# Attention and tail of a three-layer kernel: ScalarE takes part of the normalising, a compressed branch in fewer VectorE operations, split tiles moved, the last down tile in quarters

## The chip, the cores and the metric

The program runs on one core of one Trainium2 chip. The metric is the device time of one execution in microseconds; the figure is the median of several runs. The core has a matrix engine (PE, TensorE), VectorE (DVE), ScalarE (ACT), GpSimd (POOL) and SyncE (SP), which only issues transfers here. Each engine runs its own list of instructions in order and waits on semaphores.

## The reference

A block of two layers (attention mixer, gated feed-forward) is followed by a third layer of another kind; 256 tokens, 1024 features, everything in float32.

```python
def hybrid_mixer(h, w_in, ...):
    ... = jnp.split(h @ w_in, IN_OFFSETS, axis=-1)
    o_a = nsa_mixer(...)      # compressed + selected + window attention, 5 heads
    o_b = dsa_mixer(...)      # 5 heads over the 64 keys that an indexer chose
    o_c = dilated_mixer(...)  # 6 heads
    return jnp.concatenate([o_a, o_b, o_c], axis=-1)
# in nsa_mixer
    hid = jax.nn.gelu(jnp.einsum('cbnf,cfh->cbnh', raw, cmp_w1))
    kv_cmp = jnp.einsum('cbnh,chd->cbnd', hid, cmp_w2)
    p_c, _ = masked_softmax(s_c, mask_c)
    o_cmp = jnp.einsum('bhtn,bnd->bthd', p_c, v_cmp)
    gs = jax.nn.sigmoid(g)
    return gs[..., 0:1] * o_cmp + gs[..., 1:2] * o_slc + gs[..., 2:3] * o_win
# the third layer ends with
    m = jnp.einsum('btf,fd->btd', jnp.square(jax.nn.relu(u @ w_up)), w_down)
    h = h + rms_norm(m, norm_mlp_post)
```

## The kernel before

**Weights.** 170 tiles of up to 128 x 2048 float32 are streamed by SP into four buffers `raw`. Each is split for PE: ScalarE copies it to `whi` (L1174, the high part, 1.9 us), and VectorE (L1599) or GpSimd (L2422, eight pieces of 256 columns) subtracts to get `wlo`. Three split tiles are held. `ahead(tile)` splits the tile two places further on in the stream, so a line such as `ahead(l, "in", 3, 1)` in ScalarE's program means the split of the first tile of the output projection. `on_pool` says which low parts GpSimd makes; in the attention these are the last input tiles and all four output tiles. SP loads into a buffer when both parts of the tile four places earlier are made. A product of float32 accuracy is three products: high x high, high x low, low x high; twelve of them (2.8 us) make half a tile for 128 tokens (`tokens_half`, L540 to L543).

**Attention of a layer** (PE's list in `attention`, with the same-named lists of ScalarE and VectorE). Work is cut in ten pairs of jobs; a job is a group of heads over 128 queries, job 2p + i being half i of pair p. Pairs 0 to 3 are the first mixer (`NS`, a selected and a window segment for each head), 4 to 6 the second (`DS`), 7 to 9 the third (`DI`). For pair p:

- `scores(p)` on PE: a bf16 product lays down the mask (L804), products of 64 rows add the scores (L810), in bank 0 for even and bank 1 for odd jobs. It waits until the exponentials of the job before have been read from the bank.
- `highest(p)` on VectorE (L1982): the negated maxima.
- `weights(p)` on ScalarE (L1322, L1318): exponentials out of the bank to SBUF (tiles `E` and `XN`), with their sums `den`.
- `divided(p)` on VectorE: reciprocal (L1994), product with the gate for `NS` (L1999), then one scaling for each segment (L2004).
- `turned(p)`: PE transposes the weights (L822) into banks 2 and 3; ScalarE (L1334) or VectorE (L2042) copies them out.
- `values(p)` on PE (L854).

Between these stand halves of input tiles (`part`), the transposition of queries and keys (`transposed`: PE L678, out by ScalarE L1217 or VectorE L1695; pairs 9 and 11 use bank 2, pairs 10 and 12 bank 3), the last value columns (`last_values`, 24 products of 256 columns, L900 to L902, and `last_values_turned`, L908), and the output projection (`out_half`), which needs the mixed values as high part (ScalarE, L1346) and low part (VectorE, `mixed`, L2033). The jobs' order on each engine is written out by hand in the source.

**Beside it** VectorE finds the chosen keys of the second mixer: `selection(t, a, b)` is b - a rounds of eight maxima (L1723) and their replacement (L1725); `select` must be over before `scores(4)`. The compressed branch is `gelu_in` (L1817 to L1823), a tanh on ScalarE (L1351), `gelu` (L1827 to L1832), `compressed` (L1839, L1840), the scores on PE (L880), `compressed_scores` (L1845 to L1853), an exponential (L1356) and `compressed_softmax` (L1858 to L1867). Its result is one more addend of `values`.

**The end.** The third layer's 16 down tiles accumulate in banks 4 to 7, one for each half of tokens t and half of columns n. For the last tile `down` runs t = 0 wholly, then t = 1, with both n in turn. ScalarE squares each bank with a sum (`post_square`, L1399), VectorE multiplies by a gain (L2050), sums (L2396), GpSimd takes the power -1/2 (L2431), VectorE adds to the stream (L2058), and SP stores. Layers 0 and 1 end with `down_quarter`, which finishes one bank at a time.

## Time and profile before

| | |
|---|---|
| median of 3 runs | 1069.06 us (1068.77 to 1070.2) |
| the profiled execution | 1067.52 us |
| its span, first to last instruction | 1066.2 us |
| granted TensorE clock over the span | 0.994 of full speed |
| PE busy | 1043.7 us, 98% of the span |
| VectorE, ScalarE, GpSimd busy | 779.5, 539.4, 242.3 us |
| attention of layer 0, of layer 1 | about 54 to 141 us, 376 to 464 us |

Profile rows give a start from the beginning of the span. Matmuls are pipelined, so that rows of PE overlap, and the time between two starts says more than a row's length. A bracket is the engine's idle time before the row, and what ended it.

### The profile page before, as it was taken

The page shows a single profiled execution, that of the slowest core. Times are in us where ns is not written, and L with a number is a line of the kernel's source. Part 1 is how long each engine was busy: PE and PEld are TensorE (multiplying, and loading weights), DVE is VectorE, ACT ScalarE, POOL GpSimd, SP SyncE. Part 2 cuts the span into 40 slices and gives each one's busy share as a digit, 9 for nine tenths or more (in the row PEclk, how much of TensorE's full clock was granted, in tenths as well). Part 3 has the DMA queues.
Part 4 walks back from the last instruction along what each step waited for, and adds up shares of the span by engine and source line. Part 5 has one row for each costly group of instructions (what it writes and reads, how often), then busy time and mean ns, then how long its engine had stood idle before and what let it go on. Part 6 is the DMA issues. An engine that isn't in the chain of part 4 may idle for free.

```text
span 1066.2 us, 14818 instructions
## 1 busy us (share of the span) xinstructions
PE 1043.7 (98%) x5722; PEld 863.9 (81%) x5722; DVE 779.5 (73%) x1256; ACT 539.4 (51%) x797; POOL 242.3 (23%) x335
## 2 busy tenths in 40 slices
PE   8999999999999999899999999999999999999997
PEld 6777788888888867688888888998788878888886
DVE  6987568788778887658877778988754558666665
ACT  5445565555555455556555546655434445434332
POOL 1262610000000271620000003128957630000000
PEclk9989999999999999999999999999999999999999
DMA  9351345645554351355655554443444555555531
GB/s 362 124 188 60 119 157 166 230 147 209 197 177 159 138 207 41 115 173 192 203 192 197 174 182 158 159 159 124 152 158 175 199 199 186 192 198 195 171 145 39
DMA packets 26709, 179.15 MB, mean 168 GB/s; under 512 B 2960, under 2 KB 2960, under 8 KB 6160
## 3 DMA queue, kind: packets, MB, share of 16 engines
q1 hardware_dynamic: 26640, 178.22, 47.4%
q8 instruction: 45, 0.74, 0.3%
q14 instruction: 24, 0.20, 0.1%
HBM read 177.16 MB, written 1.05 MB: 167 GB/s over the span
## 4 chain that ended last, share of the span: by engine, by line
PE 90%; DVE 7%; ACT 2%; issue 1%; DMA 1%; SPq 0%; DVEq 0%; ACTq 0%
PE pb L602 18%; PE pb L603 9%; PE pb L540 8%; PE pb L541 8%; PE pb L543 7%; PE pb L628 6%; PE pb L630 6%; PE pb L629 6%; PE pb L607 3%; PE pb L854 2%; PE pb L565 1%; PE pb L566 1%; PE pb L567 1%; PE pb L606 1%; PE pb L822 1%; PE pb L810 1%
## 5 line engine op out<-in xcount | busy, mean ns | idle before, releaser
L1599 DVE TENSOR_TENSOR wlo<-raw,whi 128x2048 fp32r<-128x2048 f32 x124 | 283.7, 2290 | 113.2 <-ACT whi L1174 113.1
L1174 ACT ACTIVATE whi<-raw 128x2048 fp32r<-128x2048 f32 (+1 forms) x165 | 305.0, 1853 | 70.8 <-PE pb L543 36.9
L602 PE MATMUL pb<-hb,whi 128*128 128x512 f32 x840 | 302.0, 399 | 0.9 <-DVE hb L1621 0.9
L2422 POOL TENSOR_TENSOR wlo<-raw,whi 128x256 fp32r<-128x256 f32 x284 | 215.4, 794 | 331.1 <-ACT whi L1174 331.0
L603 PE MATMUL pb<-hb,wlo 128*128 128x256 f32 x840 | 235.9, 281 | 0.0
L602 PEld LDWEIGHTS pb<-hb,whi 128*128 128x128 f32 x840 | 158.2, 188 | 35.1 <-issue 1.1
L603 PEld LDWEIGHTS pb<-hb,wlo 128*128 128x128 f32 x840 | 159.2, 190 | 5.1
L540 PE MATMUL pb<-whi,hb 128*128 128x512 f32 x384 | 156.4, 407 | 6.0 <-DVE hb L2033 1.6
L541 PE MATMUL pb<-wlo,hb 128*128 128x512 f32 x384 | 151.3, 394 | 0.0
L543 PE MATMUL pb<-whi,hb 128*128 128x512 f32 x364 | 143.5, 394 | 0.0
L628 PE MATMUL pb<-whi,gh 128*128 128x512 f32 x288 | 114.1, 396 | 0.0
L630 PE MATMUL pb<-whi,gl 128*128 128x512 f32 x288 | 114.0, 396 | 0.0
L629 PE MATMUL pb<-wlo,gh 128*128 128x512 f32 x288 | 114.0, 396 | 0.0
L2431 POOL TENSOR_TENSOR sm<-sm 128x1 f32<-128x1 f32 x12 | 8.5, 721 | 429.0 <-DVE sm L1607 243.6
L540 PEld LDWEIGHTS pb<-whi,hb 128*128 128x128 f32 x384 | 73.1, 190 | 28.4 <-issue 13.6
L541 PEld LDWEIGHTS pb<-wlo,hb 128*128 128x128 f32 x384 | 73.2, 191 | 14.1
L543 PEld LDWEIGHTS pb<-whi,hb 128*128 128x128 f32 x364 | 69.2, 190 | 15.0
L630 PEld LDWEIGHTS pb<-whi,gl 128*128 128x128 f32 x288 | 54.2, 188 | 13.0
L629 PEld LDWEIGHTS pb<-wlo,gh 128*128 128x128 f32 x288 | 54.2, 188 | 13.0
L628 PEld LDWEIGHTS pb<-whi,gh 128*128 128x128 f32 x288 | 54.2, 188 | 11.7 <-issue 0.3
L1305 ACT ACTIVATE gh<-th 128x512 fp32r<-128x512 f32 x22 | 13.9, 632 | 76.3 <-DVE th L1958 76.3
L607 PE MATMUL pb<-hb,whi 128*128 128x512 f32 x120 | 47.5, 396 | 0.0
(367 smaller groups left out, 1472.0 us busy)
## 6 DMA issues: line engine op xcount, KB each, us to landing
raw<-wst SPq DMA_DIRECT2D x160, 1024.0 KB, 4.8
raw<-wst SPq DMA_DIRECT2D x8, 512.0 KB, 3.5
gb<-gains SPq DMA_DIRECT2D x3, 512.0 KB, 5.8
X<-x SPq DMA_DIRECT2D x4, 256.0 KB, 6.8
out<-X SPq DMA_DIRECT2D x4, 256.0 KB, 2.0
PQ<-prm SPq DMA_DIRECT2D x1, 909.0 KB, 4.5
prmt<-prm SPq DMA_DIRECT2D x1, 547.0 KB, 5.8
raw<-wst SPq DMA_DIRECT2D x2, 256.0 KB, 6.9
```

Of the source, the lines that this page charges most:

```text
L540: e.matmul(o, high[:, s], wh[:, k, :], start=first and k == 0, stop=False)
L541: mm = e.matmul(o, high[:, s], wl[:, k, :], start=False, stop=False)
L543: mm = e.matmul(o, low[:, s], wh[:, k, :], start=False, stop=last and k == 3)
L602: e.matmul(both, wh[:, k, s], hb2[:, k, :, :].rearrange("p i q -> p (i q)"), start=k == 0, stop=False)
L603: e.matmul(high, wl[:, k, s], hh[:, k, :], start=False, stop=False)
L607: mm = e.matmul(both, wh[:, 7, s], hb2[:, 7, :, :].rearrange("p i q -> p (i q)"), start=False, stop=True)
L628: e.matmul(o, ah, wh[:, k, c], start=j == 0 and k == 0, stop=False)
L629: e.matmul(o, ah, wl[:, k, c], start=False, stop=False)
L630: mm = e.matmul(o, al, wh[:, k, c], start=False, stop=last and k == 1)
L1174: e.activation(whi[:, split_slot(m), 0:w], raw[:, m % RAW, 0:w], ACT.Copy).then_inc(*hi(m))
L1599: e.tensor_tensor(wlo[:, split_slot(m), 0:w], raw[:, m % RAW, 0:w], whi[:, split_slot(m), 0:w].bitcast(F32), ALU.subtract).then_inc(*lo_v(m))
L2422: g = e.tensor_tensor(wlo[:, split_slot(m), s], raw[:, m % RAW, s], whi[:, split_slot(m), s].bitcast(F32), ALU.subtract)
```

## The change

- `divided`: for the first mixer VectorE multiplies the sum by (1 + exp(-g)) and takes one reciprocal. Then for `NS` jobs 1, 2, 3, 5 and 7 (`norm_done`) ScalarE does the scalings, in a `divided(p)` of its own in its list; VectorE goes on with jobs 0, 4 and 6 and all others.
- Compressed branch: gelu's input in two fused operations that read the bank, clamp and subtraction in one (the sign is turned, the exponential has scale -1), clamp and gate in one. The gates' reciprocal (L1781) is gone.
- VectorE's rounds of selection stand at other places among these.
- In ScalarE's list the splits behind `ahead(l, "in", 3, 1)` and `ahead(l, "in", 5, 0)` stand later, and pair 5's exponentials stand around `turned(4)`, job 10's before, job 11's behind it.
- PE does `last_values` before `values(5)` and no longer behind `turned(6)`.
- The last down tile of the third layer runs through `down_quarter`, in the order (0,0), (0,1), (1,0), (1,1); the squares wait for their own quarter.

```diff
@@ -434,6 +434,11 @@
+        def norm_done(j):
...
+            return normed_a if jobs[j][0] == NS and (j % 2 or len(jobs[j][2]) == 1 and jobs[j][1] == 0) else normed
...
         def segments(j):
@@ -632,17 +638,19 @@
-                m = tile_at[l, "down", 10, 0]
+                j = LAST_DOWN[l]
+                m = tile_at[l, "down", j, 0]
                 wh, wl = (w.rearrange("p (k c) -> p k c", k=2) for w in parts(m))
...
                 for k in range(2):
-                    e.matmul(o, gh[:, 0, k, s], wh[:, k, c], start=False, stop=False)
-                    e.matmul(o, gh[:, 0, k, s], wl[:, k, c], start=False, stop=False)
-                    mm = e.matmul(o, gl[:, 0, k, s], wh[:, k, c], start=False, stop=k == 1)
+                    e.matmul(o, gh[:, j % 2, k, s], wh[:, k, c], start=False, stop=False)
+                    e.matmul(o, gh[:, j % 2, k, s], wl[:, k, c], start=False, stop=False)
+                    mm = e.matmul(o, gl[:, j % 2, k, s], wh[:, k, c], start=False, stop=k == 1)
                 mm.then_inc(*(used(m) if t and n else half_used(m, t, n)))
-                free[DOWNB[t, n]] = x_new[("down", l), t, n]
+                if l < 2:
+                    free[DOWNB[t, n]] = x_new[("down", l), t, n]
@@ -816,7 +824,7 @@
-                        q.wait_ge(*normed[l, j])
+                        q.wait_ge(*norm_done(j)[l, j])
@@ -952,10 +960,10 @@
                 scores(7)
+                last_values()
                 values(5)
...
                 free[4], free[5] = mix_hl[l, 0], mix_hl[l, 1]
-                last_values()
                 scores(8)
@@ -1153,7 +1161,9 @@
                         down(tile_at[2, "down", j - 1, 0], j - 1, False)
-                down(tile_at[2, "down", 15, 0], 15, True)
+                for t in range(2):
+                    for n in range(2):
+                        down_quarter(2, t, n)
@@ -1306,8 +1316,8 @@
             def attention(l, transposed, project):
-                def weights(p):
-                    for j in halves_of(p):
+                def weights(p, i=None):
+                    for j in halves_of(p) if i is None else halves_of(p)[i:i + 1]:
                         k, t, hs = jobs[j]
@@ -1323,6 +1333,17 @@
+                def divided(p):
+                    for j in halves_of(p):
+                        if norm_done(j) is normed:
+                            continue
+                        n = 128 * (jobs[j][1] + 1)
+                        q.wait_ge(*divisor[l, j])
+                        for i, s in enumerate(columns(j)):
+                            o = weights_at(j)[:, i * n:i * n + n]
+                            a = e.activation(o, o, ACT.Copy, scale=co[:, s:s + 1])
+                        a.then_inc(*normed_a(l, j))
...
                 def turned(p):
@@ -1351,31 +1372,35 @@
                 ahead(l, "in", 2, 1)
+                divided(0)
                 weights(1)
-                q.wait_ge(*cmp_v[l, "less max"])
-                e.activation(ce, ce, ACT.Exp).then_inc(*act(l, "ce"))
+                q.wait_ge(*cmp_v[l, "below max"])
+                e.activation(ce, ce, ACT.Exp, scale=-1.0).then_inc(*act(l, "ce"))
+                divided(1)
                 project(2, 0, 6)
...
                 ahead(l, "in", 3, 0)
+                divided(2)
                 q.wait_ge(*mm_ce[l])
...
                 transposed(9)
+                divided(3)
                 turned(2)
...
                 project(3, 1, 7)
-                ahead(l, "in", 3, 1)
-                weights(5)
+                weights(5, 0)
                 turned(4)
+                weights(5, 1)
                 transposed(11)
                 weights(6)
+                ahead(l, "in", 3, 1)
                 turned(5)
-                ahead(l, "in", 5, 0)
                 weights(7)
@@ -1383,6 +1408,7 @@
                 turned(6)
+                ahead(l, "in", 5, 0)
                 weights(8)
@@ -1578,7 +1604,7 @@
                     for c in range(2):
-                        post_square("post2", t, c, lambda t, n: (used if t else half_used)[tile_at[2, "down", 15, 0]])
+                        post_square("post2", t, c, lambda t, n: last_down(2, t, n))
@@ -1776,9 +1802,7 @@
                 q.wait_ge(*gate_exp[l])
-                e.tensor_scalar(gs, gs, 1.0, None, ALU.add).then_inc(*dve())
-                q.wait_ge(*q.prev)
-                e.reciprocal(gs, gs).then_inc(*dve(l, "gates"))
+                e.tensor_scalar(gs, gs, 1.0, None, ALU.add).then_inc(*dve(l, "gates"))
                 e.memset(E[:, 0:2, 0:272], 0.0).then_inc(*dve(l, "E zero"))
@@ -1813,17 +1837,17 @@
                 def gelu_in():
+                    hp = PB[4][:, 256:288]
                     q.wait_ge(*mm_kv[l, "hidden"])
-                    e.tensor_copy(hx, PB[4][:, 256:288]).then_inc(*cmp_v(l, "hx"))
+                    e.tensor_copy(hx, hp).then_inc(*cmp_v(l, "hx"))
                     q.wait_ge(*q.prev)
-                    e.tensor_tensor(h2, hx, hx, ALU.mult).then_inc(*dve())
+                    e.scalar_tensor_tensor(h2, hp, 0.044715, hx, ALU.mult, ALU.mult).then_inc(*dve())
                     q.wait_ge(*q.prev)
-                    e.tensor_scalar(h2, h2, 0.044715, 1.0, ALU.mult, ALU.add).then_inc(*dve())
-                    q.wait_ge(*q.prev)
-                    e.tensor_tensor(h2, h2, hx, ALU.mult).then_inc(*cmp_v(l, "gelu in"))
+                    e.scalar_tensor_tensor(h2, h2, 1.0, hp, ALU.add, ALU.mult).then_inc(*cmp_v(l, "gelu in"))
...
                     q.wait_ge(*tanh_h[l])
+                    q.wait_ge(*cmp_v[l, "hx"])
                     e.scalar_tensor_tensor(h3, h3, 1.0, hx, ALU.add, ALU.mult).then_inc(*dve())
@@ -1848,41 +1872,38 @@
                     q.wait_ge(*q.prev)
-                    e.tensor_scalar(cm, cm, -1e29, None, ALU.max).then_inc(*dve())
-                    q.wait_ge(*q.prev)
-                    e.tensor_tensor(cev, cev, cmv.unsqueeze(3).broadcast_to([128, 2, 5, 16]),
-                                    ALU.subtract).then_inc(*cmp_v(l, "less max"))
+                    e.scalar_tensor_tensor(cev, cmv.unsqueeze(3).broadcast_to([128, 2, 5, 16]), -1e29, cev, ALU.max,
+                                           ALU.subtract).then_inc(*cmp_v(l, "below max"))
...
                     q.wait_ge(*q.prev)
-                    e.tensor_scalar(cd, cd, 1e-30, None, ALU.max).then_inc(*dve())
+                    q.wait_ge(*dve[l, "gates"])
+                    e.scalar_tensor_tensor(cdv, cdv, 1e-30, g0[:, :, :, 0], ALU.max, ALU.mult).then_inc(*dve())
                     q.wait_ge(*q.prev)
...
                     q.wait_ge(*q.prev)
-                    q.wait_ge(*dve[l, "gates"])
-                    e.tensor_tensor(cdv, cdv, g0[:, :, :, 0], ALU.mult).then_inc(*dve())
-                    q.wait_ge(*q.prev)
                     e.tensor_tensor(cev, cev, cdv.unsqueeze(3).broadcast_to([128, 2, 5, 16]),
...
                 gelu_in()
+                selection(1, 2, 3)
                 highest(0)
                 gelu()
-                selection(1, 2, 3)
+                selection(1, 3, 4)
                 compressed()
                 divided(0)
-                selection(1, 3, 4)
                 highest(1)
                 compressed_scores()
+                divided(1)
                 selection(1, 4, 6)
-                divided(1)
                 compressed_softmax()
                 highest(2)
-                selection(1, 6, 8)
+                selection(1, 6, 7)
                 divided(2)
+                selection(1, 7, 8)
                 highest(3)
@@ -1989,15 +2010,19 @@
                             at_ = at_[0:1]
-                        cv_ = co[:, at_[0]:at_[-1] + 1]
+                        cv_, dv_ = co[:, at_[0]:at_[-1] + 1], den[:, at_[0]:at_[-1] + 1]
                         q.wait_ge(*exped[l, j])
-                        e.reciprocal(cv_, den[:, at_[0]:at_[-1] + 1]).then_inc(*dve())
+                        if k == NS:
+                            q.wait_ge(*dve[l, "gates"])
+                            e.tensor_tensor(cv_.rearrange("p (h b) -> p h b", b=2), dv_.rearrange("p (h b) -> p h b", b=2),
+                                            g0[:, t, hs[0]:hs[-1] + 1:2, 1:3], ALU.mult).then_inc(*dve())
+                            q.wait_ge(*q.prev)
+                            e.reciprocal(cv_, cv_).then_inc(*divisor(l, j))
+                            if norm_done(j) is normed_a:
+                                continue
+                        else:
+                            e.reciprocal(cv_, dv_).then_inc(*dve())
                         q.wait_ge(*q.prev)
-                        if k == NS:
-                            cw_ = cv_.rearrange("p (h b) -> p h b", b=2)
-                            q.wait_ge(*dve[l, "gates"])
-                            e.tensor_tensor(cw_, cw_, g0[:, t, hs[0]:hs[-1] + 1:2, 1:3], ALU.mult).then_inc(*dve())
-                            q.wait_ge(*q.prev)
                         w = 3 * n if k == DI else n
@@ -2386,10 +2411,8 @@
                 ahead(2, "down", 15, 0)
-                post_gain("post2", 0, 0, 48)
                 for t in range(2):
-                    if t:
-                        post_gain("post2", 1, 0, 48)
+                    post_gain("post2", t, 0, 48)
                     q.wait_ge(*squares["post2", t, 1])
...
                     zz = norm_of["post2"]
```

**ScalarE, the first two pairs of the attention, and what follows them.** L1322 (L1332 now) are exponentials, L1174 (L1184) a split, L1351 (L1372) the tanh, L1356 (L1378) the compressed exponential, L1209 (L1219) an eviction of a projection, L1344 the scaling. Before:

```order
L1322 ACTIVATE E,sm<-pb,sm 128x128 x8
L1174 ACTIVATE whi<-raw 128x2048
L1322 ACTIVATE E,sm<-pb,sm 128x128 x2
L1322 ACTIVATE E,sm<-pb,sm 128x256 x2
L1356 ACTIVATE sm<-sm 128x160
L1209 ACTIVATE PQ<-pb,sm 128x512 x2
```

With the change:

```order
L1332 ACTIVATE E,sm<-pb,sm 128x128 x8
L1184 ACTIVATE whi<-raw 128x2048
L1344 ACTIVATE E<-E,sm 128x128 x4
L1332 ACTIVATE E,sm<-pb,sm 128x128 x2
L1332 ACTIVATE E,sm<-pb,sm 128x256 x2
L1378 ACTIVATE sm<-sm 128x160
L1344 ACTIVATE E<-E,sm 128x128 x2
L1344 ACTIVATE E<-E,sm 128x256 x2
L1219 ACTIVATE PQ<-pb,sm 128x512 x2
```

Four scalings stand in front of the second pair's exponentials, four more in front of the two evictions.

**ScalarE, pairs 5 to 7.** L1334 (L1355) copies turned weights, L1217 (L1227) transposed queries and keys, L1382 (L1407) the last values, L1346 (L1367) makes the mixed values' high part. Before:

```order
L1174 ACTIVATE whi<-raw 128x2048
L1322 ACTIVATE XN,sm<-pb,sm 128x128 x5
L1334 ACTIVATE PT<-pb 128x512
L1217 ACTIVATE PQ<-pb 128x256 x2
L1322 ACTIVATE E,sm<-pb,sm 128x256
L1334 ACTIVATE XN<-pb 128x256
L1174 ACTIVATE whi<-raw 128x2048
L1322 ACTIVATE E,sm<-pb,sm 128x256 x4
L1382 ACTIVATE rl<-pb 64x256
L1346 ACTIVATE hb<-pb 128x2x256 x2
```

With the change:

```order
L1332 ACTIVATE XN,sm<-pb,sm 128x128 x2
L1355 ACTIVATE PT<-pb 128x512
L1332 ACTIVATE XN,sm<-pb,sm 128x128 x3
L1227 ACTIVATE PQ<-pb 128x256 x2
L1332 ACTIVATE E,sm<-pb,sm 128x256
L1184 ACTIVATE whi<-raw 128x2048
L1355 ACTIVATE XN<-pb 128x256
L1332 ACTIVATE E,sm<-pb,sm 128x256 x4
L1407 ACTIVATE rl<-pb 64x256
L1367 ACTIVATE hb<-pb 128x2x256 x2
L1355 ACTIVATE PT<-pb 128x256
L1184 ACTIVATE whi<-raw 128x2048
```

The first split moved from ahead of the five exponentials to behind the one of pair 6; they are two and three now, with the copy between; the second split went from pair 6 to behind the mixed values.

**PE, from pair 7's scores to the first output products.** Each engine row of L900 to L902 stands for one product of the last value columns; the rest of the 24 are alike. Before:

```order
L804 MATMUL pb<-mskt 128x512 x2
L810 MATMUL pb<-PQ 128x256 x4
L854 MATMUL pb<-XN,PQ 64x128 x5
L822 MATMUL pb<-prmt,E 128x128 x2
L900 MATMUL pb<-hb,whi 64x256
L901 MATMUL pb<-hb,whi 64x256
```

With the change:

```order
L812 MATMUL pb<-mskt 128x512 x2
L818 MATMUL pb<-PQ 128x256 x4
L908 MATMUL pb<-hb,whi 64x256
L909 MATMUL pb<-hb,whi 64x256
L910 MATMUL pb<-hb,wlo 64x256
```

The value products of pair 5 (L854) and the first turning of pair 6 (L822) stood ahead of the last value columns and now stand behind them.

## Rows read from the trace of the kernel before

**Rows 1.** The page's part 1: busy us, share, instructions of an engine.
```profile
PE 1043.7 (98%) x5722; PEld 863.9 (81%) x5722; DVE 779.5 (73%) x1256; ACT 539.4 (51%) x797; POOL 242.3 (23%) x335
```

**Rows 2.** Waits of PE by line and releaser: us in total, times, longest.
```profile
PE pb L804 <- ACT E L1322: 2.4, 4, 0.9
PE pb L822 <- DVE PQ L1695: 1.9, 2, 1.0
PE pb L540 <- DVE hb L2033: 1.6, 2, 0.8
...
PE pb L678 <- ACT PT L1334: 1.4, 2, 0.7
...
PE pb L804 <- ACT XN L1322: 1.0, 2, 0.5
```

**Rows 3.** Stretches of one us, PE alone: stretch, PE busy, granted clock, DMA share, GB/s.
```profile
66.00:67.00 1.00, 1.00 (x4) 0.92 0.95 393
73.00:74.00 1.00, 1.00 (x4) 0.66 0.97 123
391.00:392.00 1.00, 1.00 (x5) 0.56 0.00 0
394.00:395.00 1.00, 1.00 (x5) 0.74 0.00 0
```

**Rows 4.** Timeline of PE, attention of layer 1: start us, us, operation, idle before.
```profile
387.94 0.39 PE L804 MATMUL pb<-mskt 128*128 128x512 bf16 x1 [0.93 <-ACT E L1322]
...
427.79 1.06 PE L678 MATMUL pb<-prmt,PQ 128*128 128x128 f32 x8 [0.71 <-ACT PT L1334]
...
432.06 0.61 PE L804 MATMUL pb<-mskt 128*128 128x512 bf16 x2 [0.32 <-ACT E L1322]
...
438.33 0.28 PE L908 MATMUL pb<-prmt,rl 64*128 64x64 f32 x2
...
439.40 0.47 PE L540 MATMUL pb<-whi,hb 128*128 128x512 f32 x1 [0.79 <-DVE hb L2033]
```

**Rows 5.** Timeline of DVE in the same attention, same columns.
```profile
382.22 0.75 DVE L1819 TENSOR_TENSOR sm<-sm 128x32 f32<-128x32 f32 x1
...
383.69 0.67 DVE L1823 TENSOR_TENSOR sm<-sm 128x32 f32<-128x32 f32 x1
...
385.47 0.27 DVE L1827 SCALAR_TENSOR_TENSOR sm<-sm 128x32 f32<-128x32 f32 x1
...
386.17 0.43 DVE L1723 MAX8 sm<-sc 128x8 f32<-128x256 f32 x1
...
386.71 0.41 DVE L1725 MATCH_REPLACE8 sc<-sm,sc 128x256 f32<-128x256 f32 x1
...
388.20 0.87 DVE L2004 TENSOR_SCALAR E<-E,sm 128x128 f32<-128x128 f32 x4
...
389.40 1.85 DVE L2004 TENSOR_SCALAR E<-E,sm 128x128 f32<-128x128 f32 x4
...
428.47 1.93 DVE L2004 TENSOR_SCALAR XN<-XN,sm 128x128 f32<-128x128 f32 x3
```

**Rows 6.** Timeline of ACT in the same attention.
```profile
384.99 0.37 ACT L1322 ACTIVATE E<-pb,sm 128x128 f32<-128x128 f32 x1 [0.37 <-DVE sm L1982]
...
387.74 1.95 ACT L1174 ACTIVATE whi<-raw 128x2048 fp32r<-128x2048 f32 x1
...
392.60 0.37 ACT L1322 ACTIVATE E<-pb,sm 128x128 f32<-128x128 f32 x1 [2.92 <-DVE sm L1982]
...
427.04 0.61 ACT L1334 ACTIVATE PT<-pb 128x512 f32<-128x512 f32 x1
```

**Rows 7.** Timeline of POOL in the same attention.
```profile
426.17 5.52 POOL L2422 TENSOR_TENSOR wlo<-raw,whi 128x256 fp32r<-128x256 f32 x8
```

**Rows 8.** Timeline of ACT at the end of the program.
```profile
1060.40 0.60 ACT L1399 ACTIVATE E<-pb 128x512 f32<-128x512 f32 x1 [1.53 <-PE pb L630]
```

11 lines of the change are left out of this document (6 added, 5 removed).

## The prediction

> **What bounds the kernel now.** I read the page's busy shares first, then who waited for whom on PE, then the granted clock in stretches of one microsecond, then the timelines of the engines in the attention of the second layer. PE is busy for 1043.7 of 1066.2 us [rows 1], so only three things are to be had: its idle time, the time at half clock, and what follows its last product. The change touches no product's size.
>
> Idle time of PE that the change can reach stands in [rows 2]: 2.4 us for the exponentials in E before score products, 1.9 for the copy of a transposed key pair (L1695), 1.6 for the low half of the mixed values (L2033), 1.4 for a weight copy (L1334), 1.0 for exponentials in XN. The first four occur in both layers and at the same places; the last is layer 1 alone. That is 8.3 us in all.
>
> The clock: it is 0.92 in the slice from 66 us and 0.66 in the one from 73 [rows 3], and 0.50 between. Two levels, 2.4 and 1.2 GHz, give the ends: from 66.84 to 73.68, so 6.8 us at half speed in layer 0, which cost 3.4. In layer 1 (0.56 and 0.74) it is 391.1 to 394.5, 3.4 us, cost 1.7. Together 5.1 us. Ahead of both falls PE had waited 0.81 and 0.93 us at the second score job, and did narrow products.
>
> **The change part by part.** All sums are against the profiled execution, 1067.5 us. That one is 1.5 us under the median of the runs shown, 1069.1; the two differ by about what one more fall of the clock costs.
>
> *The gelu's input, and the round of selection ahead of it.* VectorE now has three operations of 32 columns behind the copy, from 382.22 to 384.27 [rows 5]: 2.05 us at 0.64 to 0.75 each, while GpSimd splits a tile. A fused operation of the same width took 0.27 at 385.47 (L1827). After the change there are two fused ones that read PSUM: 0.6 us with gaps. The bounds are 0.27 and 0.75 each, so 0.6 to 1.6; I take 0.6, since the row of the same operation is nearest. One round of selection (L1723 and L1725, 386.17 to the end of the row at 386.71 and a short gap) costs 0.96 and now stands ahead of the maxima. They begin at 383.8 and not 384.27. The eight exponentials, 384.99 to 387.74 [rows 6], then end 0.5 earlier, and the second score job waits 0.3 to 0.45 and not 0.81 and 0.93 [rows 4]. **Gain 0.5 a layer, 1.0.** With the fused operations at 0.75 it is a loss of 0.5 a layer.
>
> *VectorE gives up five of its scaling jobs to ScalarE.* These are jobs 1, 2, 3, 5 and 7, and with them goes row 389.40, 1.85 us for four 128x128 scalings; the same four took 0.87 at 388.20 [rows 5]. Between the two GpSimd began a split. After the change VectorE reaches the maxima of the third pair of jobs some 3.5 us sooner: 1.85 of job 1, about 2 of jobs 2 and 3, less what stays. It only matters where PE waited for it. In layer 1 that is the 1.0 us for exponentials in XN [rows 2]; in layer 0 PE was late itself, at half clock. **Gain 1.0.** The gates' reciprocal, the clamp and the product with the gate in the compressed branch (three small operations, 0.17 to 0.5 each) are hidden: no wait of PE's in [rows 2] belongs to the transposition of that branch.
>
> ScalarE takes 4 + 2 scalings 128 wide and 6 of 256. An exponential of 128 columns with its accumulator read comes each 0.34 us (2.75 over 8) [rows 6]; that is the ceiling. The floor is nothing below a copy without accumulator, which I set at 0.25. I take 0.30, and 0.40 for 256: 1.8 + 2.4 = 4.2 us a layer. The room: ScalarE idled 2.92 us for VectorE ahead of the second pair's exponentials [rows 6]. Four scalings of job 1 are 1.2 and fit there; the others sit in front of evictions that PE needs one 12-product half later. Costed at nothing; without that cover it is 8.4 us, see the rivals.
> The Trainium skill (ScalarE: Activation LUTs, "Rules for kernel authors") speaks against this step: multiplications belong on VectorE. Its figures ("What ACT_TABLE_LOAD costs": 186 ns, 93 more for a pointer operand, 0.833 a column, 93 overlapped) would give an estimate of 0.29 and 0.40 us, so the same 4.2. As to single operations the rule agrees with the 0.22 of VectorE at 388.20; for the time of the kernel only the queue that is late counts, and that was VectorE's.
>
> *The split of the first output tile behind pair 6, pair 5's exponentials cut in two.* Now five exponentials of jobs 10 and 11 run, and only at 427.04 the copy that frees bank 2 [rows 6]. With three exponentials put behind it (3 x 0.34) it ends 1.0 earlier, at 426.6, before PE asks at 427.08 (row 427.79 less its 0.71): the 0.7 us wait (half of the 1.4) goes. Behind it VectorE scales job 11 in 1.93 us (428.47, three operations) [rows 5] while GpSimd splits that same output tile (426.17, 5.52 us) [rows 7]. That split now starts some 6 us later. Three at the uncontended 0.22 are 0.65, job 10 gains 1.0 likewise, so the copy of key pair 12, for which PE waited 0.95 (half of L1695's 1.9), is 2.0 earlier. What is late next is the exponential of job 12, behind the same copy: the 0.32 us wait before row 432.06 [rows 4] keeps some 0.25. **Gain 0.7 + 0.95 + 0.1, I take 1.9 with the rounding of the hand-off, 3.8 for both layers;** bounds 0.7 (VectorE still contended) and 2.0 a layer.
>
> *What that pays.* Call T the start of the score products at 432.06. PE has 6.55 us of work from there to the end of row 438.33 [rows 4], whatever the order, and then wants the output tile. ScalarE splits it from T on, 1.9 us, and GpSimd needs 5.5 [rows 7]: ready at T + 7.5, so PE waits 1.0 where it waited 0.79 (row 439.40). The last values moved ahead of values(5) only take the mixed values off that path (ready at T + 6.5). **Loss 0.2 a layer, 0.4.** The second output tile is ready at T + 13.5; ahead of it PE has two halves of output products (2.8 us each) and 2.8 us of narrow ones after T + 7.5, so it asks at T + 15.9 and does not wait. SP's queue loads the tile four places on behind each split, so those loads move by some 8 us; PE needs them over 20 us after T.
>
> *The last down tile in quarters.* The same 24 products. Both banks of the second half of the tokens ended together, and ScalarE squared them one after the other from 1060.40, 0.60 us each [rows 8]. The first can now be squared under the last six products. **Gain 0.5** (0 to 0.6: VectorE may be busy with the first half's sum).
>
> Sum: 1.0 + 1.0 + 3.8 - 0.4 + 0.5 = 5.9 us. From 1067.5 this is 1061.6, from the median 1063.2. I have no row that says which clock history a typical run has, and forecast the middle: **1062.4**. The bounds of the single terms give 1059.5 to 1066.
>
> **The rivals.**
> *The clock stays up.* If the shorter wait at the second score job is enough, up to 5.1 us more come back: 1057.3. For it: the falls followed just those waits. Against: they were under 1 us, and what remains is 0.3 to 0.45 beside the same narrow products, 1.3 us and more of them. By the Trainium skill (TensorE: Matmul & The Clock Gate, "Why this matters for your kernels") it is long idle gaps that lower the clock, and nothing here would count as one; [rows 3] already contradict that. Chance 0.10.
>
> *The clock falls at a new place.* Before the first output products PE would now run values(5), the score products of pair 8 and three small turnings, some 2 us, and then wait 1.0 us: that looks like the stretch ahead of 391. One fall costs 1.7, in both layers 3.4: 1065.8. Chance 0.15.
>
> *Most of the gain was hidden anyway.* Only the tail, the first 1.0 and the 0.7s arrive, and the loss: 1067.5 - 2.5, with the median's offset 1066. Chance 0.10.
>
> *ScalarE becomes the late engine, slower than before.* Its scalings stand in a queue in which each waits for a reciprocal of VectorE, which waits for ScalarE's own exponentials; behind them stand the next exponentials and the evictions of the projections. If none of it finds room, 8.4 us come on, the gain of 1.0 in XN goes, and 1062.4 becomes 1071.8. It decides at the point where the 2.92 us are less than 1.2 plus the wait for the reciprocal, that is if VectorE has job 1's reciprocal later than 1.7 us after the split ends. Against: by my account it comes 0.1 us after it. Chance 0.05.
>
> **How the numbers follow.** Forecast 0.60, clock up 0.10, new fall 0.15, mostly hidden 0.10, ScalarE late 0.05. About 0.2% (2.1 us) is what a measurement of this kernel can tell from no change, so "faster" means under 1066.9. The forecast, the clock case and nearly all of the new fall lie there, with some of the hidden case: 0.87. Same 0.08, slower 0.05. The range 1058.0 to 1066.3 reaches into the clock case and takes in the new fall.
>
> **What would show it.** Right: PE's waits for L1695 and for L1334 gone in both layers, XN's gone in layer 1; the three scalings of job 11 at 0.2 us each; a wait of about 1 us before the first output products, ended by GpSimd and not by VectorE; ScalarE's squares at the end 0.6 apart from PE's last product only once; scalings on ScalarE at 0.3 and 0.4. Wrong: half clock for more than 10 us in all, PE waiting for ScalarE's scalings (a transposition in the second block of four waits), or VectorE's maxima of the first pair no earlier than before.

## The result, and the profile after

The changed kernel takes 1058.3 us (median of 4 runs, 1056.8 to 1059.9); the kernel before took 1068.9 beside it (4 runs, 1067.6 to 1070.2). The ratio is 0.990, 95% interval 0.988 to 0.992: 10.6 us faster. The prediction was 1062.4 with a range from 1058.0: the direction was right, the size was 4 us short, and the median lies only 0.3 us inside the range; two of the four executions (1056.8 and 1057.7) lie below it. Part of that is luck, as the part on the prediction says.

The profiled execution of after is its slowest, 1059.87 us with a span of 1058.6; that of before was one of its faster ones, 1067.5. Between these two lie 7.65 us. The page's part 1, the counterpart of [rows 1]:

```profile
PE 1041.7 (98%) x5722; PEld 861.7 (81%) x5722; DVE 766.1 (72%) x1224; ACT 548.2 (52%) x821; POOL 243.2 (23%) x335
```

The waits of PE, against [rows 2] (us in total, times, longest):

```profile
PE pb L546 <- POOL wlo L2445: 1.6, 2, 0.8
...
PE pb L812 <- ACT E L1332: 1.0, 4, 0.3
...
PE pb L546 <- ACT E L1328: 0.8, 2, 0.4
```

The waits for the transposed key pair, for the copy that frees bank 2 and for the exponentials in XN are gone. The wait ahead of the first output products is ended by GpSimd. The last line is new: the third half of the output products (`out_half(1, 0, 0)`) waits for the exponentials of the last pair of jobs.

The granted clock, against [rows 3] (same columns):

```profile
66.00:67.00 1.00, 1.00 (x8) 0.79 0.65 270
67.00:68.00 1.00, 1.00 (x7) 0.50 0.00 0
...
73.00:74.00 1.00, 1.00 (x8) 0.80 0.69 229
391.00:392.00 1.00, 1.00 (x11) 1.00 0.00 0
394.00:395.00 1.00, 1.00 (x6) 1.00 0.56 205
```

Layer 0's fall is still there in this execution, 6.8 us long; layer 1's is gone. The timelines of layer 1, against [rows 4 to 7], DVE, then ACT, then PE:

```profile
380.07 0.19 DVE L1844 SCALAR_TENSOR_TENSOR sm<-pb,sm 128x32 f32<-128x32 f32 x1
380.30 0.19 DVE L1846 SCALAR_TENSOR_TENSOR sm<-sm,pb 128x32 f32<-128x32 f32 x1
...
421.86 0.68 DVE L2029 TENSOR_SCALAR XN<-XN,sm 128x128 f32<-128x128 f32 x3
```

```profile
387.90 1.28 ACT L1344 ACTIVATE E<-E,sm 128x128 f32<-128x128 f32 x4 [1.09 <-DVE sm L2020]
389.08 0.35 ACT L1332 ACTIVATE E<-pb,sm 128x128 f32<-128x128 f32 x1
...
398.15 0.91 ACT L1344 ACTIVATE XN<-XN,sm 128x256 f32<-128x256 f32 x2 [0.32 <-DVE sm L2020]
398.96 0.36 ACT L1387 ACTIVATE PQ<-pb 80x256 f32<-80x256 f32 x1
```

```profile
424.19 0.60 PE L812 MATMUL pb<-mskt 128*128 128x512 bf16 x2 [0.32 <-ACT E L1332]
...
431.68 0.47 PE L546 MATMUL pb<-whi,hb 128*128 128x512 f32 x1 [0.81 <-POOL wlo L2445]
```

The two fused operations of the gelu's input take 0.19 us each; three scalings of job 11 take 0.68, where [rows 5] had 1.93; on ScalarE, from the first of a group to whatever follows, a scaling takes 0.30 (1.18 for four) at 128 columns and 0.41 (0.81 for two) at 256. The first output products begin 7.49 us after T, and the working had T + 7.5. The third half of the output products begins 15.84 us after T before, and 16.64 after:

```profile
447.90 0.48 PE L540 MATMUL pb<-whi,hb 128*128 128x512 f32 x1
```

```profile
440.83 0.47 PE L546 MATMUL pb<-whi,hb 128*128 128x512 f32 x1 [0.41 <-ACT E L1328]
```

### The profile page after: what moved, and what is told of

The parts are those of the page before. It is cut to its first block, busy times and chain, and to the rows that moved or that the text cites. A ratio compares the mean times of both kernels' runs of the same rounds, so it can differ in the third digit from the quotient of the medians.

```text
span 1058.6 us, 14810 instructions
## 1 busy us (share of the span) xinstructions
PE 1041.7 (98%) x5722; PEld 861.7 (81%) x5722; DVE 766.1 (72%) x1224; ACT 548.2 (52%) x821; POOL 243.2 (23%) x335
## 4 chain that ended last, share of the span: by engine, by line
PE 90%; DVE 6%; ACT 3%; issue 1%; DVEq 0%; ACTq 0%
PE pb L608 19%; PE pb L609 9%; PE pb L546 8%; PE pb L547 7%; PE pb L549 7%; PE pb L634 6%; PE pb L636 6%; PE pb L635 6%; PE pb L613 3%; PE pb L862 2%; PE pb L571 1%; PE pb L573 1%; PE pb L572 1%; PE pb L612 1%; PE pb L818 1%; PE pb L511 1%
## 5 line engine op out<-in xcount | busy, mean ns | idle before, releaser
L1184 ACT ACTIVATE whi<-raw 128x2048 fp32r<-128x2048 f32 (+1 forms) x165 | 305.1, 1853 | 71.0 <-PE pb L549 36.5
L634 PE MATMUL pb<-whi,gh 128*128 128x512 f32 x280 | 110.8, 396 | 0.0
L636 PE MATMUL pb<-whi,gl 128*128 128x512 f32 x280 | 110.8, 396 | 0.0
L635 PE MATMUL pb<-wlo,gh 128*128 128x512 f32 x280 | 110.7, 396 | 0.0
```

The costliest lines, as they stand in the source:

```text
L634: e.matmul(o, ah, wh[:, k, c], start=j == 0 and k == 0, stop=False)
L635: e.matmul(o, ah, wl[:, k, c], start=False, stop=False)
L636: mm = e.matmul(o, al, wh[:, k, c], start=False, stop=last and k == 1)
L1184: e.activation(whi[:, split_slot(m), 0:w], raw[:, m % RAW, 0:w], ACT.Copy).then_inc(*hi(m))
```

## The experiments

All were timed in five rounds beside the kernel before, whose median was 1068.1 to 1069.4 in the four sets. Medians hide one thing: executions of one kernel lie at several levels, some 2 to 4 us apart, and the mean clock tends to be lower at the upper ones (0.992 to 1.0). So the clock is given with the times.

By the intervals of the ratios such a median is known to some 1.7 us only. The profiles tell more if the time is counted between PE's own products. Cut each attention in two: stretch A from the mask of the first score job (59.08 and 381.81 us in the kernel before) to the first value product of pair 3 (99.59 and 422.48), and stretch B from there to the third half of the output products (125.15 and 447.90). A holds the compressed branch, ScalarE's share and every fall of the clock in an attention; B holds the late part. In us, layer 0 and layer 1:

| kernel | A | half clock in it | B |
|---|---|---|---|
| before | 40.5, 40.7 | 6.8, 3.4 | 25.56, 25.42 |
| changed | 39.9, 36.8 | 6.8, 0 | 24.38, 24.39 |
| changed, again | 38.4, 36.8 | 3.4, 0 | 24.38, 24.39 |
| late part undone | 38.4, 36.8 | 3.4, 0 | 25.41, 25.57 |
| ScalarE's share undone | 39.4, 39.8 | 3.4, 0 | 24.39, 24.40 |
| gelu's input and selection as before | 39.0, 37.1 | 3.4, 0 | 24.39, 24.39 |
| before, wait filled | 40.6, 41.2 | 0, 0 | 25.58, 25.44 |
| that with ScalarE's share | 37.5, 37.5 | 0, 0 | 25.41, 25.56 |
| changed, wait filled | 37.4, 37.4 | 0, 0 | 24.39, 24.36 |
| dense products ahead | 38.3, 38.3 | 0, 0 | 24.38, 24.39 |
| first low half on VectorE | 38.4, 36.8 | 3.4, 0 | 24.37, 24.38 |
| that with the wait filled | 37.4, 37.4 | 0, 0 | 24.39, 24.39 |
| first shares on ScalarE too | 37.4, 37.3 | 0, 0 | 23.08, 23.12 |
| quarters alone | 43.3, 41.6 | 6.8, 0 | 25.41, 25.43 |

At the same clock, a stretch that an edit does not touch repeats within 0.2 us from kernel to kernel. Outside of A and B the profiles differ without a cause that they show: the loads at the start by some 0.5 us, and the third layer by up to 1.6.

**The changed kernel again.** No edit.

> The changed kernel once more, for more executions of both kernels with their granted clocks. Theory W (waits and clock): the change takes away 5.9 us of PE's waits and tail; the rest of the 10.6 us between the medians is that the clock falls less often, so executions of before list a mean clock of 0.990 to 0.994 and executions of this one 0.996 to 1.000; about 1058 us. Rival (clock has no part): both lists of clocks look alike and the traces differ by 10 us of PE's waits.

1058.7 us (1057.2 to 1059.6, five executions at a clock of 0.997 to 1.0), ratio 0.9902 (0.9886 to 0.9918). The result repeats. One expectation failed: the kernel before was to list clocks of 0.990 to 0.994 and listed 0.995 to 0.997. The means, 0.9956 and 0.9978, put 2.4 us of the 10.0 between the medians down to the clock. This is an estimate: half clock for t us costs t/2 us and lowers the mean over 1065 us by t/2 parts in 1065, so 0.0022 of the mean are 2.4 us. In its profile layer 0's fall is 3.4 us long, half of the other's:

```profile
67.00:68.00 1.00, 1.00 (x8) 0.71 0.05 16
68.00:69.00 1.00, 1.00 (x3) 0.50 0.00 0
...
70.00:71.00 1.00, 1.00 (x4) 0.58 0.00 0
71.00:72.00 1.00, 1.00 (x6) 1.00 0.00 0
```

**The late part undone.**

```diff
                 scores(7)
-                last_values()
                 values(5)
...
-                weights(5, 0)
+                ahead(l, "in", 3, 1)
+                weights(5)
...
```

> The changed kernel with the late part undone: ScalarE's splits, pair 5's exponentials and PE's last value columns as before. Theory W: PE's waits for the copy of pair 4 (0.7), for key pair 12 (0.95) and for the mixed values (0.8) come back in both layers, the 0.8 us for GpSimd's low half goes: 3.4 us slower than the changed kernel, about 1061.7 us. Rival (the gain is in the first half of the attention and the clock): within 1 us of 1058.3.

1062.4 us (1061.5 to 1062.8). The waits of [rows 2] are back: 2.0 us for the key pair, 1.6 for the mixed values' low half, 1.4 for the copy; those of POOL and of the last exponentials (2.4) are gone. The medians are 3.7 us apart, where the terms said 3.8 - 0.4 = 3.4. But stretch B, the only one that the edit changes, is longer by 1.03 and 1.18 us, together 2.2; the two other pairs of kernels that differ in the late part (before and changed, ScalarE's share on top of the filling and the filled changed kernel) give 2.2 as well. So the late part is worth 2.2. The rest of the 3.7 does not lie in the attentions and has no shown cause; in this one profile PE also waits 1.6 us for VectorE once in the third layer, which the edit does not touch.

**ScalarE's share undone**: all scalings on VectorE.

```diff
-            return normed_a if jobs[j][0] == NS and (j % 2 or len(jobs[j][2]) == 1 and jobs[j][1] == 0) else normed
+            return normed
```

> The changed kernel with all scalings on VectorE again. Theory W: VectorE reaches the maxima of the third pair some 3.3 us later, where the changed kernel has a margin of 0.1 us in layer 1, so PE waits up to 3 us in each layer: 1061 to 1064 us. Rival (only layer 1's 1.0 us hung on it, as the prediction had it): 1059.3 us. Rival (ScalarE's share does nothing): 1058.3 us.

1062.8 us (1061.7 to 1063.9) at a clock of 0.997 to 1.0. The share is worth 4.1 us, four times its term. Stretch A agrees, 4.0 us longer, and says where: 1.0 in layer 0, in which the clock fell for 3.4 us in both kernels, and 3.0 in layer 1, at full clock. Waits of PE in this kernel:

```profile
PE pb L812 <- ACT XN L1332: 1.6, 3, 0.6
...
PE pb L896 <- DVE sm L1887: 1.2, 1, 1.2
```

The second is PE waiting for the compressed branch's softmax, which the prediction called hidden: [rows 2] have no such wait. VectorE in the same kernel, layer 1: the second job's four scalings under GpSimd's split take 2.60 us, and the next maxima begin at 389.77 (387.78 in the changed kernel).

```profile
386.06 0.87 DVE L2029 TENSOR_SCALAR E<-E,sm 128x128 f32<-128x128 f32 x4
...
387.25 2.60 DVE L2029 TENSOR_SCALAR E<-E,sm 128x128 f32<-128x128 f32 x4
389.77 1.01 DVE L2003 TENSOR_REDUCE sm<-pb 128x2 f32<-128x256 f32 x2
```

**The gelu's input and the rounds of selection as before.**

```diff
-                    e.scalar_tensor_tensor(h2, hp, 0.044715, hx, ALU.mult, ALU.mult).then_inc(*dve())
+                    e.tensor_tensor(h2, hx, hx, ALU.mult).then_inc(*dve())
+                    q.wait_ge(*q.prev)
+                    e.tensor_scalar(h2, h2, 0.044715, 1.0, ALU.mult, ALU.add).then_inc(*dve())
...
                 gelu_in()
-                selection(1, 2, 3)
                 highest(0)
...
```

> The changed kernel with the gelu's input in its old operations and the rounds of selection at their old places. Theory W: the exponentials end 0.5 us later, the second score job waits 0.7 and not 0.2: 1.0 us for both layers, and if that wait is what lets the clock fall, 1.7 to 3.4 us more in the mean: 1059.3 to 1062.7 us. Rival (the clock does not hang on that wait): 1059.3 us with a mean clock as in the changed kernel.

1059.9 us, but its six executions run from 1056.5 (clock 0.999) over 1059.8 to 1060.0 (three, 0.995 and 0.996) to 1064.6 and 1064.7 (both 0.992). PE waits 0.80 and 0.53 us at the second score job, against 0.20 in both layers of the changed kernel, and stretch A is longer by 0.6 and 0.3: the predicted direct gain of 1.0 is there, at 0.9, though the fastest execution (0.3 below the fastest of the changed kernel) hides it. Whether the shorter wait also keeps the clock up is open. Levels at 0.992 and 0.995 did not occur in the nine executions of the changed kernel, but the profiled one here has 0.995 from two falls of 3.4 us, and only one of them is in the attention, where the changed kernel has one too. The other, at 11.3 us, stands in the first input tiles, ahead of all that this edit touches.

**The wait filled, in the kernel before.** Four products that serve nothing, ahead of the second job's mask.

```diff
+                        if j == 3:
+                            bank_free(2)
+                            for _ in range(4):
+                                e.matmul(PB[2][:, :], hh[:, 0, 0:128], hb2[:, 0, :, :].rearrange("p i q -> p (i q)"),
+                                         start=True, stop=True)
```

> The kernel before, with four products of 512 columns put in that serve nothing (their result is overwritten), ahead of the mask of the second score job in both attention layers, where TensorE waited 0.81 and 0.93 us. They are 0.9 us of work, so they fill the wait and add nothing beside it. Theory C (the clock falls behind that wait, because TensorE stood still there): the falls become rarer or shorter in both layers, mean clock 0.998 or more, and the time goes from 1068.7 to 1063 to 1066, though the kernel does more work. Rival N (the falls have to do with the narrow products behind, not with the wait): the falls stay, mean clock 0.995 to 0.996, time 1068.5 to 1069.5.

1068.0 us (12 executions), the same as before within 0.13% (interval 0.9988 to 1.0013). Theory C holds for the clock, in the profile of one execution: at both places of [rows 3] it stays at 2.4 GHz.

```profile
66.00:67.00 1.00, 1.00 (x4) 1.00 0.95 401
...
391.00:392.00 1.00, 1.00 (x7) 1.00 0.00 0
394.00:395.00 1.00, 1.00 (x10) 1.00 0.00 0
```

It fails for the time. Seven of the twelve executions have a clock of 0.999 or 1.0, and they take 1066.8 to 1068.2; the five at 0.993 to 0.996 take 1069.5 to 1072.5. Getting back 5.1 us of clock leaves the best executions where those of the kernel before are (1066.7). Its waits say why:

```profile
PE pb L893 <- DVE sm L1872: 2.7, 2, 1.4
PE pb L809 <- ACT XN L1327: 2.2, 4, 0.6
```

At full clock PE arrives earlier, and VectorE is late in both layers: 4.9 us where the kernel before showed 1.0. Half clock and a late VectorE cover each other: stretch A is as long without a fall (40.6 and 41.2) as with it (40.5 and 40.7).

**ScalarE's share on top of the filling**: the changed kernel with the late part and the early part undone, and the four products in.

> The kernel before with ScalarE's share of the scalings, the compressed branch in fewer operations and the quarters at the end, and with the four filling products; the gelu's input, the rounds of selection and the late part as before. With the filling alone, the clock stayed up in the profile of the kernel before, and VectorE turned up late in its place: 2.7 us for the compressed softmax and 2.2 for the exponentials in XN over both layers. Theory W (the share takes just these waits away, and was hidden in the kernel before only because TensorE was slower at half clock): 4.5 to 5 us less than with the filling alone, of which the quarters are 0.5, so 1062 to 1063, both waits gone and the clock at 0.999. Rival (the share is worth 1.0 as predicted, whatever the clock does): 1067.3 minus 1.5, 1065.8.

1059.9 us (1059.2 to 1061.0). Both waits just shown are gone; those that are left at these places are the late part's.

```profile
PE pb L835 <- DVE PQ L1725: 1.9, 2, 1.0
PE pb L546 <- DVE hb L2064: 1.6, 2, 0.8
...
PE pb L686 <- ACT PT L1360: 1.4, 2, 0.7
...
PE pb L817 <- ACT E L1337: 1.1, 2, 0.5
```

The profiled spans, both at a clock of 0.999, are 1065.5 and 1059.7: 5.8 less, of which 4.9 are the two waits and 0.5 the tail. Medians say more (1067.2 for the seven at full clock, so 7.3); the profiled one is the slowest of the six here. The attentions say the same as the medians: stretch A is shorter by 3.1 and 3.7, together 6.8 (from start to start a wait costs more than its listed idle time), and 1.4 of it is lost again in the third layer of this profile. Theory W's mechanism holds and the rival (1065.8) falls; the gain is larger than forecast. It is not ScalarE's share alone: the compressed branch in fewer operations came with it and has no run of its own. The share alone, undone above, was 3.0 in layer 1 at full clock, so the other operations may be worth up to 0.7 there.

**The wait filled, in the changed kernel.** Same edit.

> The changed kernel with the same four products. The wait there is only 0.2 to 0.3 us now, so without an effect on the clock they cost 0.6 to 0.7 us a layer, 1.2 to 1.4: 1058.7 goes to 1060.0 (rival N). Theory C: the fall that is left in layer 0 (2 to 6 us at half clock, 1 to 3.4 us of time) goes, mean clock 1.0 in all executions, and the time is 1057 to 1058.5, with a narrower spread.

1056.9 us (1056.5 to 1057.2), ratio 0.989 (0.9873 to 0.9907), the clock 0.999 in all four executions and 1.0 in both attentions. Eight products more, 1.8 us less, and a spread of 0.6 instead of 3. The intervals of the two ratios overlap, so the size is not certain; in stretch A the filling costs 0.6 us where the clock had not fallen (layer 1) and gives back 1.0 or 2.5 where it had for 3.4 or 6.8 us (layer 0), so 0.5 to 2.0 in all.

```profile
66.00:68.00 2.00, 2.00 (x13) 1.00 0.53 221
68.00:70.00 2.00, 2.00 (x12) 1.00 0.00 0
```

**Dense products ahead of the narrow ones.**

```diff
                 scores(1)
-                compressed_scores()
                 part(2, 1, 1)
+                compressed_scores()
```

> The changed kernel with the twelve products of 512 columns of the projection put ahead of the compressed branch's six narrow score products (they stood behind). Theory C2 (it is the run of narrow products behind a short wait that lets the clock fall, and 2.8 us of wide ones in between prevent it): layer 0's fall goes, minus 1 to 3.4 us. Against that the compressed scores come 2.8 us later, VectorE waits some 1 us for them, and the exponentials in XN of layer 1, which had 0.1 us to spare, become late again by up to 1 us. Together 1056.5 to 1058. If the clock does not care for the order: 1059 to 1060.

1059.0 us (1058.3 to 1059.4), clock 0.998 to 1.0. The stretches from 66 to 72 us stay at 1.00 with the short wait of 0.20 us ahead of them as it was; but a new wait costs 3.1 us, half of it in each layer, since ScalarE's eviction stands behind the exponential of the compressed scores, which now come later:

```profile
PE pb L546 <- ACT PQ L1219: 3.1, 2, 1.6
```

Expected was the late XN; what came was a wait for ScalarE's queue. The gain of the clock, 1.7, is paid back: against the changed kernel's second profile stretch A is 0.1 shorter in layer 0 and 1.6 longer in layer 1. That the order kept the clock up is likely and not shown: it is one profile, and the changed kernel has executions at 1.0 too.

**The first output tile's low half on VectorE.**

```diff
-                return name == "out" or name == "in" and j in (2, 3, 5)
+                return name == "out" and (j, plan[m][4]) != (0, 0) or name == "in" and j in (2, 3, 5)
...
                 highest(7)
+                split(tile_at[l, "out", 0, 0])
                 mixed(0)
```

> The changed kernel with the low half of the first output tile made by VectorE in one operation (2.3 us, between the maxima of pair 7 and the low halves of the mixed values, where VectorE stood idle for 3.0 us) and not by GpSimd in eight (5.6 us). If the wait of 0.8 us ahead of the first output products is GpSimd's alone, it goes in both layers: minus 1.6 us, 1058.7 becomes 1057.1, and no other wait appears over 0.3 us. Rival: VectorE is late with the low half of the mixed values instead, or the loads behind that tile meet other traffic, and the wait stays under another name: 1058.4 to 1059.

1057.4 us (1056.0 to 1059.4, clock 0.997 to 0.999). GpSimd's wait is gone, and another grew:

```profile
PE pb L546 <- ACT E L1328: 2.1, 2, 1.1
```

The third half of the output products begins at 439.72 us here and at 440.83 in the changed kernel, whose whole attention stands 1.11 us later (score products of pair 8 at 428.63 and 429.74). Counted from there both begin at the same moment. The 0.64 us won at the first products are lost at the third half.

**Both, filling and VectorE's low half.** No edit of its own.

> The changed kernel with both the filling products and the low half of the first output tile on VectorE. In the profile of the latter alone the first output products began 0.64 us earlier, counted from the same score products, but the next output half began at the same time, since it waited 1.06 us instead of 0.41 for the exponentials of the last pair. Theory M (VectorE's chain of shares and last maxima sets that stretch, so GpSimd's lateness costs nothing): same as with the filling alone, 1056.9, within 0.3. If the two gains add: 1055.3 to 1055.8.

1057.3 us (1056.9 to 1058.6), 0.4 above the filled kernel, where 0.3 was allowed, and 1.5 above the other theory's range. Stretch B decides it: 24.39 in both layers with VectorE's low half, 24.39 and 24.36 without. Theory M; GpSimd's lateness costs nothing.

**Shares of the first half on ScalarE too.** As the last, and:

```diff
+            if j in (2 * THIRD - 2, 2 * THIRD):
+                return normed_a
...
                 ahead(l, "out", 0, 0)
+                q.wait_ge(*dve[l, "both shares"])
+                for j, c, g in ((2 * THIRD - 2, 0, 0), (2 * THIRD - 2, 1, 1), (2 * THIRD, 0, 2)):
+                    w = weights_at(j)[:, 256 * c:256 * c + 256]
+                    a = e.activation(w, w, ACT.Copy, scale=f6[:, g:g + 1])
+                    if g:
+                        a.then_inc(*normed_a(l, j))
                 weights(9)
...
+                        if i == 0:
+                            e.tensor_scalar(f, f, z, None, ALU.mult).then_inc(*dve(l, "both shares"))
+                            continue
```

> As the one with both, and the three scalings by the shares of the first half of the last two heads go to ScalarE, which stands idle for 4.2 us there; VectorE only multiplies the three shares by the reciprocal. By theory M VectorE's last maxima come some 1.8 us earlier and the 1.06 us wait for the last exponentials goes in both layers, with the 0.8 of GpSimd's gone already: 1056.9 minus 2 times 0.7 to 1.1, so 1054.7 to 1055.5. Rival (the wait belongs to something else, or the maxima now wait for the score products, which end only then): 1056.5 to 1057.

**1054.5 us (1054.2 to 1055.3), ratio 0.9874 (0.9858 to 0.9890)**: the fastest kernel of this study; even its slowest execution is below the changed kernel's fastest (1056.8). ScalarE in the kernel without this edit, then with it:

```profile
438.71 0.58 ACT L1333 ACTIVATE E<-pb,sm 128x384 f32<-128x384 f32 x1 [4.21 <-DVE sm L2006]
```

```profile
432.64 0.92 ACT L1425 ACTIVATE E<-E,sm 128x256 f32<-128x256 f32 x2
433.44 0.52 ACT L1425 ACTIVATE XN<-XN,sm 128x256 f32<-128x256 f32 x1
434.81 0.58 ACT L1335 ACTIVATE E<-pb,sm 128x384 f32<-128x384 f32 x1 [0.85 <-DVE sm L2014]
```

ScalarE stood idle for 4.21 us, waiting for maxima that VectorE could not take before its own scalings. Three of them moved, some 1.3 us of ScalarE's time, and the exponentials begin 3.9 us earlier (2.2 counted from the first output products, at 429.73 and 428.00). The third half of the output products starts 8.50 us behind the first and not 9.80, with no wait: 1.3 a layer, 2.6, and the medians differ by 2.8.

**The quarters alone, in the kernel before.**

```diff
-                down(tile_at[2, "down", 15, 0], 15, True)
+                for t in range(2):
+                    for n in range(2):
+                        down_quarter(2, t, n)
```

> The kernel before with only the last down tile taken by quarters of the sums. Theory: one of ScalarE's two squares at the end (0.60 us) leaves the path, minus 0.5 us, so 1068.2 becomes 1067.7, in the profile only one square behind the last product; the clock is not touched, so the executions keep their levels between 1066 and 1071. Rival: the quarters shift the closing additions of VectorE too, and with them up to 1.5 us: 1066.7.

1067.7 against 1068.1 us, interval of the ratio 0.9988 to 1.0012: too small to time. The profile has it:

```profile
1062.44 0.60 ACT L1403 ACTIVATE E<-pb 128x512 f32<-128x512 f32 x1 [0.71 <-PE pb L644]
...
1063.84 0.60 ACT L1403 ACTIVATE E<-pb 128x512 f32<-128x512 f32 x1 [0.71 <-PE pb L644]
```

Each square now has its own quarter ahead of it, 1.40 us apart, and one alone stands behind PE's last product. From its start to the end of the span it is 5.3 us (1069.1 - 1063.84). Before, from the first of the two in [rows 8], it was 5.8 (1066.2 - 1060.40). The same execution has a lesson on the clock. Here it did not fall at 66 us, though the wait for the exponentials was there; PE then waited 1.41 us for the compressed softmax and 0.58 and 0.48 for XN, and the clock fell at 80:

```profile
80.00:82.00 2.00, 1.52 (x4) 0.50 0.02 4
...
84.00:86.00 2.00, 2.00 (x7) 0.50 0.83 315
86.00:88.00 2.00, 2.00 (x10) 0.80 0.99 410
```

In layer 1 of the same execution the wait is there again, with no filling and no fall behind it (the granted clock from 380 to 420 us is 1.00). There too PE then stands still for the compressed softmax, and stretch A is longer than before although the clock stayed up, 41.6 against 40.7:

```profile
390.42 0.39 PE L806 MATMUL pb<-mskt 128*128 128x512 bf16 x1 [0.73 <-ACT E L1326]
...
404.25 0.42 PE L890 MATMUL pb<-prmt,sm 128*80 128x128 f32 x2 [1.62 <-DVE sm L1871]
```

So in this profile the attention as it was, with nothing put in, shows the hidden wait where the clock stays up.

## Why the prediction was right, and where it was short

*Gelu's input and selection, 1.0.* Confirmed in place: PE waits 0.2 us at the second score job, not 0.81 and 0.93. The operations took 0.19 each, less than the 0.27 taken. Stretch A of layer 0, with a fall of 6.8 us in both profiles, is 0.6 shorter; undoing the step costs 0.9 over both layers.

*ScalarE's scalings, 1.0, hidden otherwise.* Here the working failed. Undone, it costs 4.1 us. ScalarE's own bill was right (0.30 and 0.41 a piece, estimated 0.30 and 0.40), and it found room. The failing step is "it only matters where PE waited for it", read from [rows 2]: in that execution PE ran 10 us at half clock just ahead of those places, and the half clock hid VectorE's lateness. The table shows it by degrees: the share gives nothing in layer 0 beside a fall of 6.8 us (the 0.6 there are the step above), 1.0 beside one of 3.4, and 3.0 beside none. That "no wait of PE's in [rows 2] belongs to the transposition of that branch" was true of the trace and false of the kernel; at full clock that wait is 1.3 us a layer. The Trainium skill (ScalarE: Activation LUTs, "Rules for kernel authors") sends multiplications to VectorE, for its speed per element. For a single operation alone this case agrees (0.22 on VectorE, 0.30 on ScalarE); beside a split by GpSimd VectorE took 0.65 (2.60 for four), and as to the kernel's time the rule is contradicted twice, by these 4.1 us and by the 2.8 of the last step.

*The late part, 3.8 less 0.4.* 2.2 measured in stretch B, so this term was 1.2 too high. Its gains came: T is 1.8 us nearer in each layer (1.9 in the sum), the three scalings took 0.68 (0.65), and T + 7.5 came out to a hundredth. The loss was mis-sized, 0.64 and 0.80 us and not 0.2 a layer. The wait for GpSimd was named correctly and is not what costs: with GpSimd out of the way the third half of the output products starts at the same moment. The failing sentence is the one on the second output tile, "so it asks at T+15.9 and does not wait". PE starts that half at T + 16.64, after a wait of 0.41 for the exponentials of the last pair, and behind these stand VectorE's shares and last maxima, which the working did not look at.

*The tail, 0.5.* Seen in the profile, 5.8 to 5.3 us, and within the noise of the runs.

*The clock.* The sum took it as unchanged, "stays up" was a rival at 0.10 and gave 1057.3. What happened lies between: layer 1's fall is gone in both profiles of the changed kernel, layer 0's is 6.8 us in one and 3.4 in the other. Profiled execution against profiled execution, 5.9 (the sum) + 1.7 (one fall less) = 7.6, and 7.65 is measured. This agreement is luck. Term by term the same two profiles give 1.3 for the gelu's input (1.0 in the sum), 1.5 for the share (1.0), 2.2 for the late part (3.4), 0.5 for the tail (0.5), 1.7 for the fall and 0.4 for loads at the start, which have nothing to do with the change. And without ScalarE's share the 1.7 would have turned into waits for VectorE, as filling the wait in the kernel before showed, so part of what is booked under clock is the share's. The other 3 us of the 10.6 come from which executions were profiled: before's was 1.4 below its median, after's 1.6 above. The clock accounts for part of that; with its estimated 2.4 us and the 5.5 of the terms, two to three us between the medians stay unassigned. The new fall before the first output products (chance 0.15), the hidden gain and a late ScalarE did not come.

## What to carry to other kernels

Read a trace's waits together with its clock: a wait list taken while TensorE runs slowly is short by what the slow stretches hide, so an edit of an engine that is "hidden" there must be costed at full clock too, and repairing the clock alone may give nothing. When a wait is removed, follow it to the next point at which the same engine has to wait; if that point does not move, nothing was won, and the engine to relieve is the one behind it. Where an engine idles for 4 us for maxima of another that is busy with multiplications, try the multiplications there, even at a higher price each. And measure a step from product to product inside the stretch that it changes: here that repeats within 0.2 us at the same clock, and the medians do not settle 1.7.

## What the runs showed of the hardware

- TensorE's clock fell to 1.2 GHz for 3.4 or 6.8 us in the attentions, after waits of 0.2 to 1.4 us with narrow products around them, and stayed up there in the five profiles in which products of 512 columns filled the wait, and in the one in which they stood ahead of the narrow ones. It is not certain in either direction: the wait was there at 65 and at 390 us in one profile (0.83 and 0.73 us) without a fall behind it, and executions of kernels without filling reach a clock of 1.0 too. The Trainium skill (TensorE: Matmul & The Clock Gate, "Why this matters for your kernels") tells of long idle gaps; no gap here was long. What exactly decides was not tried.
- TensorE did more work in less time: with eight wide products that serve nothing the changed kernel took 1.8 us less in the median (0.5 to 2.0 by stretch A) and had a spread of 0.6 us.
- VectorE slows down beside GpSimd: four 128x128 scalings took 0.87 us alone and 2.60 across a split by GpSimd, in one kernel within 2 us. Two operations of 32 columns that read one operand from PSUM took 0.19 each at 380.07, while GpSimd was in a split (378.44 to 384.01); with both operands in SBUF the old ones took 0.67 and 0.75 beside such a split [rows 5]. The operand's place was not varied alone.
